# Second token tile laid backwards, one score product per head and scan level

## What is computed

```python
b = jnp.cumsum(gc, axis=2)                       # gc = log g, per token and feature
diff = b[:, :, :, None, :] - b[:, :, None, :, :]
decay = jnp.exp(jnp.where(causal[:, :, None], diff, -jnp.inf))
scores = jnp.einsum('bhtk,bhtsk,bhsk->bhts', qc, decay, kc)
o_intra = jnp.einsum('bhts,bhsv->bhtv', scores, vc)
...
z = u @ w_in                                     # the input projection, 2048 x 11264
s = jnp.einsum('bhnqd,bhnkd->bhnqk', qb, kb) * (Dh ** -0.5) + bias[:, None]
```

## Time and profile before

| | us |
|---|---|
| median of 3 runs | 1961.11 (1960.43 to 1963.77) |
| the profiled execution, its time | 1963.14 |
| the profiled execution, its span | 1961.4 |
| TensorE busy in the span | 1932.9 (99%) |
| VectorE / ScalarE / GpSimd busy | 1122.7 / 898.6 / 190.3 |
| 128 level products of line 482, levels 0 to 7 | 8 stretches of 3.57 each |
| 8 products of level 8, line 486 | 1.78 |

### The profile page before, as it was taken

The page is one execution under the profiler, slowest core; times in us unless marked ns, Lnnn a source line. Parts: engine busy times, 40 slices in busy tenths (PEclk is TensorE's granted clock), DMA queues, the critical chain, the costliest instruction groups (busy, mean ns, idle before and its releaser), DMA issues.

```text
span 1961.4 us, 34129 instructions
## 1 busy us (share of the span) xinstructions
PE 1932.9 (99%) x13560; PEld 1785.4 (91%) x13560; DVE 1122.7 (57%) x1219; ACT 898.6 (46%) x1156; POOL 190.3 (10%) x111
## 2 busy tenths in 40 slices
PE   8999999999999999999999999999999999998998
PEld 8989998898899988998998899899889998888986
DVE  6657887456645555554445444554565446766664
ACT  6533333366544444443444344334454344664553
POOL 1002443200000100000000000001000001031000
PEclk9999999999999999999999999999999999999999
DMA  8655555565465566655665656565556554344454
GB/s 258 189 175 155 176 156 152 168 179 153 143 209 194 178 217 183 194 192 192 193 194 191 186 181 192 193 190 186 182 183 179 176 172 135 107 137 137 133 190 142
DMA packets 175990, 345.36 MB, mean 176 GB/s; under 512 B 10816, under 2 KB 11024, under 8 KB 175328
## 3 DMA queue, kind: packets, MB, share of 16 engines
q1 hardware_dynamic: 174160, 337.76, 55.6%
q0 software_dynamic: 1696, 5.64, 1.0%
HBM read 341.26 MB, written 2.10 MB: 175 GB/s over the span
## 4 chain that ended last, share of the span: by engine, by line
PE 96%; DVE 2%; ACT 1%; issue 0%; DMA 0%; SPq 0%; POOL 0%; DVEq 0%; ACTq 0%
PE ps L398 57%; PE ps L410 31%; PE ps L482 1%; DVE wlo L1159 1%; PE ps L711 1%; ACT whi L804 1%; PE ps L698 1%; PE ps L675 0%; PE ps L539 0%; PE ps L529 0%; PE ps L428 0%; PE ps L521 0%; PE ps L520 0%; DMA x_nat<-in_x_dram 0%; PE ps L686 0%
## 5 line engine op out<-in xcount | busy, mean ns | idle before, releaser
L1159 DVE TENSOR_TENSOR wlo<-raw,whi 128x1024 fp32r<-128x1024 f32 x632 | 818.8, 1302 | 737.0 <-ACT whi L804 736.1
L804 ACT ACTIVATE whi<-raw 128x1024 fp32r<-128x1024 f32 x632 | 665.4, 1058 | 929.9 <-PE ps L398 592.5
L398 PE MATMUL ps<-xhi,whi 128*128 128x256 f32 (+1 forms) x1984 | 571.7, 288 | 0.0
L398 PE MATMUL ps<-xlo,whi 128*128 128x256 f32 (+1 forms) x1984 | 560.0, 282 | 0.0
L398 PE MATMUL ps<-xhi,wlo 128*128 128x256 f32 (+1 forms) x1984 | 559.8, 282 | 0.0
L398 PEld LDWEIGHTS ps<-xhi,whi 128*128 128x128 f32 x1984 | 376.1, 190 | 12.9 <-issue 11.9
L398 PEld LDWEIGHTS ps<-xlo,whi 128*128 128x128 f32 x1984 | 375.9, 189 | 1.6 <-issue 0.7
L398 PEld LDWEIGHTS ps<-xhi,wlo 128*128 128x128 f32 x1984 | 375.3, 189 | 0.0
L398 PE MATMUL ps<-x2lo,whi 128*128 128x256 f32 x1024 | 285.2, 279 | 1.5 <-issue 1.5
L398 PE MATMUL ps<-x2hi,whi 128*128 128x256 f32 x1024 | 285.4, 279 | 0.2 <-issue 0.2
L398 PE MATMUL ps<-x2hi,wlo 128*128 128x256 f32 x1024 | 285.2, 279 | 0.0
(11 more groups left out here) (335 smaller groups left out, 2241.3 us busy)
## 6 DMA issues: line engine op xcount, KB each, us to landing
raw<-in_w_in_dram SPq DMA_DIRECT2D x280, 512.0 KB, 3.8
raw<-in_w_up_dram SPq DMA_DIRECT2D x128, 512.0 KB, 3.7
raw<-in_w_down_dram SPq DMA_DIRECT2D x128, 512.0 KB, 3.8
raw<-in_w_out_dram SPq DMA_DIRECT2D x64, 512.0 KB, 3.9
raw<-in_w_branch_a_dram SPq DMA_DIRECT2D x16, 512.0 KB, 5.3
raw<-in_w_branch_b_dram SPq DMA_DIRECT2D x16, 512.0 KB, 4.3
x_nat<-in_x_dram SPq DMA_DIRECT2D x4, 512.0 KB, 7.2
rel<-in_rel_bias_dram POOLq DMA_DIRECT2D x8, 256.0 KB, 4.0
```

Of the source, the lines that this page charges most:

```text
L398: ins = mm(outs[b], w[:, k % SLOTS, j, cols], v[:, kt, 0:n], start=start, stop=last and j == CK - 1 and i == 2, skip_group_check=True)
L804: f(whi[:, k % SLOTS], raw[:, k % SLOTS], ACT.Copy).then_inc(whi_ready, 1)
L1159: tt(wlo[:, k % SLOTS], raw[:, k % SLOTS], whi[:, k % SLOTS], ALU.subtract).then_inc(wlo_ready, 1)
```

## The change

The second token tile is laid backwards: token 255 comes first, token 128 last. The host lays `x`, the position tables and the distances so, and turns the output back. In a backward tile the later half of each block of 2·hb stands first. So the earlier halves of tile 0 and those of tile 1 fill complementary places, and so do the later halves. In each level from 1 to 7:

- ScalarE copies the earlier halves of both tiles into one tile of keys for each head, `k_both`: two copies of 128 x 512 for a level (`k_gather`), after the last split of the group before. They wait for `k_decay` of the level before.
- TensorE multiplies it with the later halves of both tiles, read in place out of `qp` with an access pattern of three steps: 8 products instead of 16. `qp` holds tile 1 in its first half and tile 0 in its second for this. Levels 0 and 8 keep their 16 and 8 products.
- `level_mask` and `level_add` work on 128 x 512 halves instead of 128 x 1024. Level 1 is written straight into the sum `pairs` and needs no add.
- `q_decay` and `k_decay` are written as two instructions, one for each tile, with the same elements in all.

In the end two triangle masks `tri`, loaded late by GpSimd, part `pairs` into the two tiles on VectorE (`unpack`, group 13 after k = 4 and 5), and GpSimd adds each to `acc` (`tile_add`), for which `hg_output` waits. The bias of the banded attention is a third piece now, from a second table loaded by a second DMA for each two heads (`rel_a`, 128 KB beside the 256 KB of `rel`), with one more VectorE instruction in a unit.

The core of the diff:

```diff
@@ level_scores, TensorE
-                if level > 1:
+                if 1 <= level < LEVELS - 1:
+                    pe.wait_ge(hg_kb, level)
+                if level == LEVELS - 1:
                     pe.wait_ge(hg_k, level - 1)
...
+                elif level < LEVELS - 1:
+                    hb = 2 ** (level - 1)
+                    both_tiles = [2 * hb, P // (2 * hb)], [P + hb, 2], [1, hb]
+                    for hd in range(HG):
+                        ins = mm(misc[:, hd // 4, (hd % 4) * P:(hd % 4 + 1) * P],
+                                 k_both[:, hd, :], spread(qp[:, hd, 0:1], *both_tiles),
+                                 start=True, stop=True)
@@ hg_output, TensorE
-                pe.wait_ge(hg_acc, 2 * (LEVELS - 2))
+                pe.wait_ge(hg_acc, 2 * (LEVELS - 3) + 2)
@@ ScalarE
+            def k_gather(level):
+                hb = 2 ** (level - 1)
+                act.wait_ge(hg_s, 1)
+                if level > 1:
+                    act.wait_ge(hg_k, level - 1)
+                for t in range(NT):
+                    ins = f(spread(k_both[:, 0, t * hb:t * hb + 1], [P, HG], [2 * hb, P // (2 * hb)], [1, hb]),
+                            spread(kr[:, 0, t * (P + hb):t * (P + hb) + 1], [T, HG], [2 * hb, P // (2 * hb)], [1, hb]),
+                            ACT.Copy)
+                ins.then_inc(hg_kb, 1)
...
+                    if G_LEVEL <= g < G_HGOUT - 2 and k == NC - 1:
+                        k_gather(g - G_LEVEL + 1)
@@ level_mask and unpack, VectorE
+                if level >= 3:
+                    dve.wait_ge(hg_acc, 2 * (level - 3) + i + 1)
+                dst = pairs if level == 1 else masked
+                tt(dst[:, heads, :], src, spread(masks[:, level, :], [0, 4], [1, P]), ALU.mult).then_inc(hg_m, 1)
+            def unpack(t):
+                dve.wait_ge(hg_acc, 2 * (LEVELS - 3))
+                dve.wait_ge(tri_in, 16)
+                tt((masked, pairs)[t][:], pairs[:], spread(tri[:, t, :], [0, HG], [1, P]), ALU.mult).then_inc(hg_u, 1)
@@ att_bias, VectorE
+                for i, bias in enumerate((ra[:, ::-1], rb[:, 0:P], rb[:, P:T][:, ::-1])):
+                    ins = stt(out=prob[:, u % 3, i * P:(i + 1) * P], in0=ps[:, 4, i * P:(i + 1) * P], scalar=-1.0,
+                              in1=bias, op0=ALU.mult, op1=ALU.subtract)
@@ GpSimd
+            def tile_add(t):
+                pool.wait_ge(hg_u, t + 1)
+                v = acc[:].rearrange("p (n t) c -> p n t c", t=NT)[:, :, t, :]
+                tt(v, v, (masked, pairs)[t][:], ALU.add).then_inc(hg_acc, 1)
...
-                tt(v, v, spread(src[:, 1:2], [2, n], [0, hb]), ALU.mult).then_inc(hg_k, 1)
+                for t in range(NT):
+                    early = t * P + t * hb
+                    late = t * P // hb + 1 - t
+                    v = spread(kr[:, 0, early:early + 1], [T, HG], [2 * hb, P // (2 * hb)], [1, hb])
+                    ins = tt(v, v, spread(src[:, late:late + 1], [T // hb, HG], [2, P // (2 * hb)], [0, hb]), ALU.mult)
+                ins.then_inc(hg_k, 1)
...
+                if g == G_HGOUT - 1:
+                    for t in range(NT):
+                        tile_add(t)
```

More of the change, by code:

```diff
@@ L164, in program @@
         acc = at("acc", 68, [P, HG * NT, P])
-        masked = at("masked", 76, [P, HG * NT, P])
+        pairs = at("pairs", 76, [P, HG, P])
+        masked = at("masked", 80, [P, HG, P])
+        tri = at("tri", 60, [P, 2, P])
+        k_both = at("k_both", 84, [P, HG, P])
         kr = at("kr", 88, [P, HG, T])
@@ L1288, in level_mask @@
                     return
-                src = misc[:, 2 * i:2 * i + 2, :].rearrange("p b (x c) -> p (b x) c", x=4)
-                if level == 0 and i == 0:
-                    dve.wait_ge(mask_in, 16)
-                if level >= 2:
-                    dve.wait_ge(hg_acc, 2 * (level - 2) + i + 1)
-                dst = acc if level == 0 else masked
-                tt(dst[:, half, :], src, spread(masks[:, level, :], [0, 8], [1, P]), ALU.mult).then_inc(hg_m, 1)
+                if level == 0:
+                    if i == 0:
+                        dve.wait_ge(mask_in, 16)
+                    tt(acc[:, 8 * i:8 * i + 8, :],
+                       misc[:, 2 * i:2 * i + 2, :].rearrange("p b (x c) -> p (b x) c", x=4),
+                       spread(masks[:, 0, :], [0, 8], [1, P]), ALU.mult).then_inc(hg_m, 1)
+                    return
@@ L1307, in q_decay @@
                     dve.wait_ge(hg_g, level - 1)
-                v = flat.rearrange("p (n two h) -> p n two h", two=2, h=hb)[:, :, 1, :]
-                tt(v, v, spread(src[:, 0:1], [2, n], [0, hb]), ALU.mult).then_inc(hg_q, 1)
+                for t in range(NT):
+                    late = (1 - t) * P + (1 - t) * hb
+                    early = t * P // hb + t
+                    v = spread(qp[:, 0, late:late + 1], [T, HG], [2 * hb, P // (2 * hb)], [1, hb])
+                    ins = tt(v, v, spread(src[:, early:early + 1], [T // hb, HG], [2, P // (2 * hb)], [0, hb]), ALU.mult)
+                ins.then_inc(hg_q, 1)
             def hg_scale(i):
@@ L1359, in _ @@
                             q_decay(level)
+                        if k in (4, 5) and level == LEVELS - 1:
+                            unpack(k - 4)
                     if g == 1 and k in (1, 3):
@@ L1684, in k_decay @@
                     tt(dst[:, 0:n], pair[:, :, 0], pair[:, :, 1], ALU.mult).then_inc(hg_g, 1)
-                v = kr[:].rearrange("p n t -> p (n t)").rearrange("p (n two h) -> p n two h", two=2, h=hb)[:, :, 0, :]
-                tt(v, v, spread(src[:, 1:2], [2, n], [0, hb]), ALU.mult).then_inc(hg_k, 1)
+                for t in range(NT):
+                    early = t * P + t * hb
[3 more added lines that the diff above has]
+                ins.then_inc(hg_k, 1)
             def bias_load(j):
@@ L1691, in bias_load @@
                     pool.wait_ge(hg_m, 2 * LEVELS)
+                    pool.wait_ge(hg_t, 2)
                 if j >= 2:
                     pool.wait_ge(at_nm, 2 * (j - 1))
[L1694 to L1699 removed]
+                for dst, w, first, n in ((rel_a, rel_bias, REL_CLIP + 1 - P, P), (rel, rel_turned, 2 * REL_CLIP + 1 - 2 * T, T)):
+                    src = bass.AP(w.tensor, w.offset + 2 * j * N_REL + first, [[1, P], [N_REL, 2], [1, n]])
+                    load(dst[:, j % 2, :, :], src).then_inc(rel_in[j % 2], 16)
+                pool.wait_ge(rel_in[j % 2], 32 * (j // 2 + 1))
+                nc.gpsimd.memset(rel_a[0:DH, j % 2, :, 0:DH], MASKED)
+                nc.gpsimd.memset(rel[DH:P, j % 2, :, T - DH:T], MASKED).then_inc(rel_ready, 1)
             for g in range(G_IN):
@@ L1703, in _ @@
                     level = g - G_LEVEL
-                    for i in range(2):
-                        level_add(level, i)
+                    if level >= 2:
+                        for i in range(2):
+                            level_add(level, i)
                     k_decay(level)
+                    if level == 2:
+                        pool.wait_ge(hg_k, 1)
+                        load(tri[:], triangles).then_inc(tri_in, 16)
+                if g == G_HGOUT - 1:
+                    for t in range(NT):
+                        tile_add(t)
                 if g == G_HGOUT:
@@ L1792, in shape_constants @@
         hb = 2 ** (level - 1)
-        masks[:, level, :] = (s // (2 * hb) == t // (2 * hb)) & ((s // hb) % 2 == 0) & ((t // hb) % 2 == 1)
+        masks[:, level, :] = (s // (2 * hb) == t // (2 * hb)) & ((s // hb) % 2 != (t // hb) % 2)
+    triangles = np.stack([s < t, s > t], axis=1).astype(f32)
     inv_freq = (f32(10000.0) ** (-np.arange(0, DH, 2, dtype=f32) / f32(DH))).astype(f32)
-    row = np.concatenate([np.arange(T) // 64, np.zeros(META, int)]).astype(f32)
-    col = np.concatenate([np.arange(T) % 64, np.zeros(META, int)]).astype(f32)
+    places = token_order()
+    row = np.concatenate([places // 64, np.zeros(META, int)]).astype(f32)
+    col = np.concatenate([places % 64, np.zeros(META, int)]).astype(f32)
     ang = np.stack([row[:, None] * inv_freq, col[:, None] * inv_freq]).astype(f32)
@@ L1820 @@
     arrays, args = {}, []
-    for name, a in [(n, inputs[n]) for n in _NAMES] + list(shape_constants().items()):
+    places = token_order()
+    constants, last = shape_constants()
+    laid = {n: inputs[n] for n in _NAMES}
+    laid["x"] = laid["x"][:, places]
+    turned = {"rel_turned": inputs["rel_bias"][:, :, ::-1]}
+    for name, a in [*laid.items(), *constants.items(), *turned.items(), *last.items()]:
         a = np.ascontiguousarray(a)
```

55 lines of the change are left out of this document (28 added, 27 removed).

## The result

The changed kernel takes 1942.7 us (median of 4 executions, 1941.4 to 1944.3) against 1960.8 us for the kernel before in the same comparison (4 executions, 1956.4 to 1963.8). The ratio is 0.9925, 95% interval 0.9911 to 0.9938. The profiled execution has a span of 1941.0 us against 1961.4 us, 20.4 us less.

What follows compares the result with a forecast made beforehand. TensorE, busy 99% of the span, was taken to bound the kernel. Seven levels saving 1.79 us each, with all added work priced 0, gave 1961.11 - 12.5 = 1948.6 us; range 1946.3 to 1953.0 us.

Steps and rivals of the forecast that it cites:

- The path term: Scan levels 1 to 7 on TensorE: 8 products instead of 16, 1.79 us saved a level, 12.5 us in all.
- The moving read: Products of levels 1 to 7 reading query columns out of two tiles: priced 0, upper end 1.8 us at level 1.
- Rival (1): Level 1's single-column reads from alternating tiles are slow: 1.8 us more if doubled, 1950.4 us; chance 0.08.
- The rule quoted: SBUF reads: full speed needs two accesses per 16-byte line; level 1 would break it, later levels not; no size stated.
- Rival (3): Gathered reads slow at all levels: 1961.1 us if product time doubles, 1973.6 us at three times; chance 0.06.
- The added work: Copies on ScalarE (1.24 us a level), group 13's unpacking and adds, and one more attention bias instruction: priced 0.
- Rival (2): Gathered keys reach TensorE late at levels 2 to 7: 1 us too long over six levels gives 1954.6 us; chance 0.08.
- rival (4): The output in group 13 waits for the second `tile_add`, 2 us at most: 1950.6 us; chance 0.04.
- the third bias instruction: In the attention, the maximum comes about 0.1 us later, with 1.3 us of room in the first unit: price 0.
- the sum's frame: Program behind the scan: bound by TensorE alike, nothing fixed to a time, so the 12.5 us gain isn't given back.

Runs made afterwards that it cites:

- `half_products`: The kernel before with levels 1 to 7 skipping the second token tile's products, all else kept: 1941.5 us, ratio 0.9920.
- `twice`: The changed kernel with each product of levels 1 to 7 issued a second time: 1961.2 us, ratio 1.001.
- `after_plus224`: The changed kernel with 112 more transposes of 16 columns (224 list entries) at the very start: 1953.9 us, or 1944.4 us less the late start.
- `before_plus32`: The kernel before with 16 more transposes of 16 columns (32 list entries) at the very start: 1954.7 us, ratio 0.9999.
- `straight`: The changed kernel with both of TensorE's loops written out: 1943.1 us in one execution.

## Why the prediction was wrong, step by step

**The path term was right.** Level products cost what level 8's cost, 1.78 us, in five of seven levels, and `half_products` shows that they are the whole gain. Direction and mechanism held.

**The moving read was mis-sized: 0 was taken, 1.0 us it is.** Level 1 costs 2.66 us and level 2 1.92 us, 0.88 + 0.14 us over. The step that failed argued from a rate ("a read at half speed would hardly show"): the row with a gap between two long runs says nothing of columns that each come from another place. Rival (1), with 1.8 us as its bound, had the mechanism and the place, at twice the size. (In the earlier trace rows the row with the gap is that of L659, 592 ns: the heading there names the two in the other order, the prediction reads them rightly.) The rule quoted, that of the 16-byte line in the Trainium skill's "Advanced Engine Details and Errata", section SBUF Cachelines, fits in part. One column per line is slow (3.63 us) and two per line aren't (1.81 us), as it says. But another line at three columns in four is free if the two places are 20 bytes apart (1.78 us), and level 2, which it lets pass, costs 0.14 us. Rival (3), cost at all levels, didn't come.

**The added work is hidden, and more easily than laid out.** ScalarE and then GpSimd in group 7 of the changed kernel (start us, us, engine, line, operation, tiles, shapes, count):

```profile
205.63 1.14 ACT L904 ACTIVATE k_both<-kr 128x512 f32<-128x512 f32 x2
```

```profile
197.87 2.03 POOL L1740 TENSOR_TENSOR g_even<-g_odd 128x512 f32<-128x512 f32 x1
199.86 3.48 POOL L1745 TENSOR_TENSOR kr<-kr,g_odd 128x512 f32<-128x512 f32 x2
```

The two copies took 1.14 us (1.24 forecast) and end at 206.8 us, 3.4 us ahead of level 3's products at 210.22 us. The decays took 3.48 us for both, not 4.06, and end at 203.3 us. With gaps in reads and writes neither engine slowed. Rival (2) had no ground: 3.4 us left, not 1.9, and 3.3 to 3.5 us at each of levels 1 to 7. The copies start behind ScalarE's own last split of the group, not behind the decays, which were done 2.3 us earlier. VectorE and then GpSimd in group 13:

```profile
348.86 1.21 DVE L1339 TENSOR_TENSOR pairs<-pairs,tri 128x1024 f32<-128x1024 f32 x1
```

```profile
350.15 3.31 POOL L1727 TENSOR_TENSOR acc<-acc,pairs 128x1024 f32<-128x1024 f32 x1 [2.30 <-DVE pairs L1339]
```

The second `tile_add` takes 3.31 us, the blocked price, and ends at 353.5 us; the output's first product stands at 355.83 us in the chain. 2.4 us are left, within the 2.2 to 3.1 us laid out, and rival (4) fell. In the first attention unit the last maximum starts 1.04 us behind the first bias, where it was 0.97 us: 0.07 us for the third bias instruction, 0.1 forecast, and TensorE has no new wait there.

**What failed is the sum's frame.** "The rest of the program is bound by TensorE in the same way and nothing in it is fixed to a time, so the gain isn't given back behind" was taken to mean that the rest costs the same. It doesn't. The time to subtract from, 1961.1 us, held some 8 us of stall and slow quarters (it is that far over the 1952.4 and 1953.0 us of the same kernel with the loop written out; within one comparison it was 3.8 and 7.3 us). They hang on the jump back and on where the loop lies in TensorE's list, and taking 224 entries (56 products of two records, each with its weight load) out of the list moved the loop. The stretch of 768 products at 90.45 us and the 1.52 us of "issue" were in the chain of the kernel before, next to stretches of 87.07 us for the same work. So was the line of 1.7 us of "issue" among TensorE's waits, of which the earlier trace rows has the two longest alone. That comparison wasn't made: I read the chain only where the change touched it. The sum by what the runs show: 11.5 us in the scan, some 1.5 us of it lost again in places that stay open, and the rest of the 18 us, about 8 us, from the quarters (8.8 us in the two profiled executions). That the changed kernel's list lies well is luck: nothing in the change aims at it. The range was drawn around the spread of three executions; a kernel whose executions span 10 us needed its lower end at least 5 us lower.

What stays argued: that both stops are fetches of instructions that the jump back makes late. The DMA queue that carries instructions (q8 in part 3 of the page) shows 106 packets, 1.74 MB or 16.4 KB each, in the four kernels whose profile has the stall behind 13 products (before, its copy, `twice`, `after_plus224`), and 103 or 104 in the other kernels with the loop, `before_plus32` among them though its list is longer than before's. (`straight`, which has neither loop, shows 106 and no stall, so the count alone decides nothing.) In the trace of before one packet is on its way from 1115.99 to 1116.87 us, and the jump back ends at 1118.4 us, 1.5 us behind it. The next is on its way from 1119.59 to 1120.47 us; the stall begins at 1120.45 us and ends at 1121.97 us, again 1.5 us behind it. In the other three kernels the stall ends 1.4 to 1.5 us behind such a packet too. Between 1134.9 and 1194.3 us one comes every 14.9 us, which is about 126 products, or 252 entries with their weight loads (an estimate from the pace of 117.8 ns). This fits blocks of 256 entries, but no run separated the fetch from the jump. Why a stretch then runs at 118 ns instead of 113 ns for 90 us isn't known either.

## What to carry to other kernels

Before pricing an edit, compare equal stretches of the chain over the whole program: where the same work takes two different times, the difference belongs to the kernel's time but not to its work, and any edit ahead of it may add or remove it. To measure what an edit is worth, write out the loop that scatters the times in both versions, or give both lists the same length. (Here that brought the difference of the times within 0.2 us of that of the stretches, twice; the 95% intervals are some 2 us to either side, so that closeness is in part luck.) In float32 products of 128 columns, a moving read with a steady step was nearly free with two columns in every 16 bytes and doubled the product with one; single columns in turn from two distant places made it half as long again.

## What was not expected of the hardware

- Eight float32 products of 128 columns take 1.78 us with the moving columns in one run, 1.81 us at every second element, 3.63 us at every fourth, 2.66 us in turn from two places 516 bytes apart, 1.78 us from two places 20 bytes apart.
- The jump back of a TensorE loop with 1152 products in its body takes 3.7 to 4.9 us in its queue, that of a loop with 192 products 0.2 us. The products already queued cover 3.9 us. The long one can be followed by a stop of 1.5 to 2.7 us behind 13 products and by a slower pace, 118 ns a product instead of 113.4 ns, that lasts for a whole stretch of 768 products at full granted clock (0.997), 3.4 us each. Kernels with the same instructions in the loop differ in the stop by where the list ahead of them puts it.
- 112 transposes of 16 columns took 11.95 us, 107 ns each.
